# A router and its experts that read x without its norm, in a two-layer recurrent trunk on one core

## The reference, cut to what is computed

```python
def rmsnorm(x, g, eps=RMS_EPS):
    xf = x.astype(jnp.float32)
    y = xf * lax.rsqrt(jnp.mean(xf * xf, axis=-1, keepdims=True) + eps)
    return (y * g.astype(jnp.float32)).astype(x.dtype)
...
def moe_swiglu(h, router, wg, wu, wd):
    probs = jax.nn.softmax((h @ router).astype(jnp.float32), axis=-1)
    top_p, top_i = lax.top_k(probs, TOP_K)
    top_p = top_p / jnp.sum(top_p, axis=-1, keepdims=True)
    gates = jnp.sum(jax.nn.one_hot(top_i, N_EXPERTS, dtype=jnp.float32) * top_p[..., None], axis=-2)
    out = jnp.zeros_like(h)
    for e in range(N_EXPERTS):
        out = out + gates[..., e:e + 1].astype(h.dtype) * swiglu(h, wg[e], wu[e], wd[e])
    return out
...
        h = rmsnorm(x, W['norm_ffn'][i])
        j = i // 2
        if i % 2 == 0:
            x = x + swiglu(h, W['ffn_w_gate'][j], W['ffn_w_up'][j], W['ffn_w_down'][j])
        else:
            x = x + moe_swiglu(h, W['moe_router'][j], W['moe_w_gate'][j], W['moe_w_up'][j],
                               W['moe_w_down'][j])
```

## Time and profile before

| what | value |
|---|---|
| median of 3 runs | 1668.62 us (1667.72 to 1671.55) |
| profiled execution, its own time | 1666.78 us |
| its span, first to last instruction | 1664.9 us |
| mean granted TensorE clock | 0.868 of full |
| busy share PE, PEld, DVE, ACT, POOL | 88, 76, 55, 45, 8% |
| HBM read, written | 225.5 MB, 8.1 MB |
| instructions | 27200 |

### The profile page before, as it was taken

The page is one execution under the profiler, slowest core; times in us unless marked ns, Lnnn a source line. Parts: engine busy times, 40 slices in busy tenths (PEclk is TensorE's granted clock), DMA queues, the critical chain, the costliest instruction groups (busy, mean ns, idle before and its releaser), DMA issues.

```text
span 1664.9 us, 27200 instructions
## 1 busy us (share of the span) xinstructions
PE 1460.6 (88%) x10452; PEld 1257.3 (76%) x10452; DVE 917.4 (55%) x1433; ACT 755.6 (45%) x1124; POOL 127.5 (8%) x160
## 2 busy tenths in 40 slices
PE   4988799897699999899788989766899999999996
PEld 3876677766699999788577776666587788778874
DVE  3644453425444444564445243543588888888885
ACT  4532323123343333462132221432477777877774
POOL 0111111010000000001201100000000000000000
PEclk9997886767899999898788676686799999999998
DMA  5321211014244444042121101320489778987981
GB/s 199 111 65 57 65 39 53 2 66 169 90 152 131 150 150 142 34 124 60 51 64 52 53 2 66 137 87 13 158 296 342 279 285 304 330 286 290 341 287 61
DMA packets 62055, 234.83 MB, mean 141 GB/s; under 512 B 7056, under 2 KB 7152, under 8 KB 61072
## 3 DMA queue, kind: packets, MB, share of 16 engines
q1 hardware_dynamic: 59328, 217.61, 38.0%
q0 software_dynamic: 2496, 13.71, 2.2%
q10 hardware_dynamic: 144, 2.28, 0.3%
HBM read 225.48 MB, written 8.09 MB: 140 GB/s over the span
## 4 chain that ended last, share of the span: by engine, by line
PE 52%; issue 33%; DVE 8%; ACT 4%; POOL 1%; DMA 1%; POOLq 0%; ACTq 0%; DVEq 0%
PE bank L492 11%; PE bank L493 10%; PE bank L494 10%; PE bank L486 7%; ACT whi L1141 1%; PE bank L506 1%; PE bank L604 1%; DVE wlo L1541 1%; PE bank L622 1%; PE bank L636 1%; PE bank L899 1%; PE bank L850 1%; DVE htmp L1556 1%; DMA x<-in_x 1%; PE bank L634 1%
## 5 line engine op out<-in xcount | busy, mean ns | idle before, releaser
L1541 DVE TENSOR_TENSOR wlo<-wraw,whi 128x1024 fp32r<-128x1024 f32 x410 | 506.5, 1238 | 345.3 <-ACT whi L1141 335.2
L1141 ACT ACTIVATE whi<-wraw 128x1024 fp32r<-128x1024 f32 x410 | 433.3, 1060 | 388.9 <-PE bank L494 294.0
L492 PE MATMUL bank<-hh,whi 128*128 128x320 f32 x968 | 333.6, 345 | 53.9 <-DVE hl L1561 36.6
L493 PE MATMUL bank<-hl,whi 128*128 128x320 f32 x968 | 321.7, 332 | 0.0
L494 PE MATMUL bank<-hh,wlo 128*128 128x320 f32 x968 | 319.9, 330 | 0.0
L492 PEld LDWEIGHTS bank<-hh,whi 128*128 128x128 f32 x968 | 202.8, 209 | 69.7 <-issue 43.3
L493 PEld LDWEIGHTS bank<-hl,whi 128*128 128x128 f32 x968 | 202.6, 209 | 0.8
L494 PEld LDWEIGHTS bank<-hh,wlo 128*128 128x128 f32 x968 | 202.2, 209 | 0.0
L1059 PE MATMUL bank<-whi,hh 128*128 128x512 f32 (+1 forms) x384 | 149.3, 389 | 1.0 <-DVE place L2072 1.0
L1061 PE MATMUL bank<-wlo,hh 128*128 128x512 f32 (+1 forms) x384 | 144.2, 376 | 0.0
L1060 PE MATMUL bank<-whi,hl 128*128 128x512 f32 (+1 forms) x384 | 144.1, 375 | 0.0
(11 more groups left out here) (377 smaller groups left out, 2127.1 us busy)
## 6 DMA issues: line engine op xcount, KB each, us to landing
wraw<-in_w SPq DMA_DIRECT2D x410, 512.0 KB, 5.0
smb<-in_s_ssm POOLq DMA_DIRECT2D x2, 1536.0 KB, 6.7
out_o_ssm<-smb POOLq DMA_DIRECT2D x2, 1536.0 KB, 5.4
cst<-in_consts ACTq DMA_DIRECT2D x1, 2225.0 KB, 12.3
srw<-in_s_rwkv POOLq DMA_DIRECT2D x2, 768.0 KB, 6.1
out_o_rwkv<-srw POOLq DMA_DIRECT2D x2, 768.0 KB, 3.6
x<-in_x SPq DMA_DIRECT2D x1, 1280.0 KB, 12.1
out_y<-x SPq DMA_DIRECT2D x1, 1280.0 KB, 4.5
```

What stands on the lines that cost most here:

```text
L492: mm(out, hi, rh, start=first, stop=False)
L493: mm(out, hi, rl, start=False, stop=False)
L1141: af(whi[:, ring % HI, :], wraw[:, POS[ring], :], ACT.Copy).then_inc(S("slot_hi"), 1)
L1541: tt(wlo[:, POS[ring], :], wraw[:, POS[ring], :], whi[:, ring % HI, :].bitcast(F32), ALU.subtract).then_inc(S("slot_split"), 1)
```

## The change

Only layer 1 from the output projection on.

* **No norm in front of the router.** ACT writes `hidh` = x g (rounded) and DVE `hidl` = x g - hidh during the output projection (`raw`, `raw_lo`); router and transposes read them, k by k. The squares are summed per token (`token_sums`: squares as weights, one column of ones, three blocks) into `rs_tok`, the factor r per token. DVE multiplies the logits by it.
* **Ranks and places token by token.** Ranks come from the logits, not from the softmax; `chosen` is rank < 1.5. TensorE counts places with the `causal` and `ones` matrices over `chosen` (`places`, 6 + 3 fp32 matmuls, between the fourth and fifth transpose unit). DVE multiplies by `chosen` into `pos9`. Exp and the gates come after the branch's inputs. The zero fills of the last block are left out, as the gather reads 64 rows there.
* **Per expert, in the loop.** Before the down slots three transposes turn `pick` into the place matrix (B[6]), DVE copies it to `place` at slot 23 and writes the next `pick` at slot 25. After the gather three matmuls of two columns (`slot_scales`) give each slot's gate x r and r; ACT copies them to `slot_g`. Silu uses r as its scale, the down result gate x r.
* ACT's and DVE's split of the third expert slot moves behind the router; the waits for the state DMAs move to DVE, in front of the first pick.
* The dense branch, not taken here, norms x itself.

The diff's core:

```diff
+            def token_sums(i, tiles):
+                for k in tiles:
+                    pe.wait_ge(S("sq_ready"), KT * i + k + 1)
+                    for q, (c0, n) in enumerate(BLOCKS):
+                        m = mm(B[q][0:n, 0:1], sqb[:, k % 2, c0:c0 + n], C("ones", 0, 1), start=(k == 0), stop=(k == KT - 1))
                     m.then_inc(S("sq_used"), 1)
...
             def router():
-                full_slot(G_FFN[L] - 1, G_FFN[L] - 1, B[6][:, 0:T])
+                pe.wait_ge(S("slot_split"), G_FFN[L])
+                for k in range(KT):
+                    pe.wait_ge(S("h_split"), KT * (2 * L + 1) + k + 1)
+                    m = three(B[6][:, 0:T], k, G_FFN[L] - 1, hidh[:, k, :], hidl[:, k, :], k == 0, k == KT - 1)
+                m.then_inc(S("slot_used"), 1)
+                token_sums(2 * L + 1, [KT - 1])
...
                 for u in range(6):
-                    if u >= 2:
-                        pe.wait_ge(S("ro_act"), (2, 3, 5, 6)[u - 2])
+                    if u < 2:
+                        pe.wait_ge(S("nrm_sd"), 2 * L + 2)
+                    else:
+                        pe.wait_ge(S("ro_act"), u)
+                    if u == 4:
+                        places()
...
+            def places():
                 pe.wait_ge(S("ro_dve"), 2)
+                of = [rt["chosen"][0:n, q, :] for q, (_, n) in enumerate(BLOCKS)]
+                for q, (_, n) in enumerate(BLOCKS):
+                    for r in range(q):
+                        mm(B[5][0:n, q * NEXP:(q + 1) * NEXP], C("ones", 0, n), of[r], start=(r == 0), stop=False)
+                    mm(B[5][0:n, q * NEXP:(q + 1) * NEXP], C("causal", 0, n, slice(0, n)), of[q], start=(q == 0), stop=True)
...
+            def slot_scales(i):
+                for q, (_, n) in enumerate(BLOCKS):
+                    of = gate_rs[0:n, q, :, i] if isinstance(i, int) else \
+                        gate_rs[0:n, q, :, bass.ds(i, 1)].rearrange("p a o -> p (a o)")
+                    m = mm(B[1][:, 256:258], pick[0:n, q, :].bitcast(F32), of,
+                           start=(q == 0), stop=(q == 2))
...
             def experts_picked():
-                gather(0)
-                for e in range(NEXP):
-                    for q in range(3):
-                        m = mm(B[5][:, e:e + 1], pick[:, e, q, :].bitcast(F32), rt["g"][:, q, e:e + 1],
-                               start=(q == 0), stop=(q == 2))
-                m.then_inc(S("ro_pe"), 1)
-                for e in range(NEXP):
-                    if e >= 2:
-                        pe.wait_ge(S("ro_dve"), 6 + e - 1)
-                    mm(B[e % 2][:, 0:T], one_of(e, NEXP), pos1[:, :],
-                       start=True, stop=True).then_inc(S("ro_pe"), 1)
+                pe.wait_ge(S("ro_dve"), 4)
+                pe.wait_ge(S("ro_act"), 7)
+                gather()
+                pe.wait_ge(S("ro_dve"), 6)
+                slot_scales(0)
...
+                    for q, (c0, n) in enumerate(BLOCKS):
+                        m = pe.transpose(B[6][:, c0:c0 + n], pick[0:n, q, :].bitcast(F32),
+                                         C("ident", 0, n, slice(0, n)))
+                    m.then_inc(S("place_pe"), 1)
                     for f in range(FT):
...
-                    gather(i + 1)
+                    pe.wait_ge(S("place_in"), 2 * i + 2)
+                    gather()
+                    slot_scales(i + 1)
```

On ACT and DVE:

```diff
+            def raw(tiles):
+                for k in tiles:
+                    act.wait_ge(S("out_read"), KT * L + k + 1)
+                    af(hidh[:, k, :], x[:, k, :], ACT.Copy, scale=V("g_ffn", k)).then_inc(S("hh_k"), 1)
+                    squares(2 * L + 1, [k])
...
+            def slot_scales(i):
+                act.wait_ge(S("taken"), 3 * i + 3)
+                if not isinstance(i, int):
+                    act.wait_ge(S("y_lo"), 2 * i)
+                af(slot_g[:, :], B[1][:, 256:258], ACT.Copy).then_inc(S("taken_hi"), 1)
...
-                            af(sil[:, c % 2, 0:n], B[c % 2][:, 0:n], ACT.Silu).then_inc(S("sil"), 1)
+                            if c == 0:
+                                act.wait_ge(S("taken_hi"), 2 * i + 2)
+                            af(sil[:, c % 2, 0:n], B[c % 2][:, 0:n], ACT.Silu,
+                               scale=slot_g[:, 1:2]).then_inc(S("sil"), 1)
...
+            def raw_lo(k):
+                v.wait_ge(S("hh_k"), KT * (2 * L + 1) + k + 1)
+                stt(hidl[:, k, :], x[:, k, :], V("g_ffn", k), hidh[:, k, :].bitcast(F32), ALU.mult, ALU.subtract)\
+                    .then_inc(S("h_split"), 1)
...
+            def picks(e):
+                at = pos9[:, :, e:e + 1] if isinstance(e, int) else pos9[:, :, bass.ds(e, 1)]
+                return tt(pick[:, :, :], rep(count_up[:, :], 3), at.to_broadcast([P, 3, P]), ALU.is_equal)
...
+                        if j == 2 * FT + 1:
+                            v.wait_ge(S("place_pe"), i + 1)
+                            cp(place[:, :], B[6][:, 0:T]).then_inc(S("place_in"), 1)
+                        if j == 2 * FT + 3:
+                            picks(i + 1).then_inc(S("place_in"), 1)
```

More of the change, by code:

```diff
@@ L365, in trunk @@
         htk = [sb("htk_" + k, [P, 3, D], F32R) for k in "hl"]
[L366 to L370, removed]
+        pick = sb("pick", [P, 3, P], F32R)
+        exp_end, top[0] = top[0], yt_at
         cmp = sb("cmp", [P, 3, NEXP, NEXP])
@@ L970, in router @@
                 m.then_inc(S("ro_pe"), 1)
[L971 to L978, removed]
+                pe.wait_ge(S("ro_act"), 9)
                 for e in range(NEXP):
@@ L1009, in experts_dense, with gather @@
                 expert_loop(pe, L, body)
-            def gather(i):
+            def gather():
                 for z, bk in enumerate((6, 2)):
                     for k in range(KT):
-                        for q in range(3):
[L1016 to L1019, removed]
-                    m.then_inc(S("taken"), 1)
@@ L1122, in _ @@
                 else:
+                    norm(2 * l + 1, range(KT - 2, KT))
+                    pe.wait_ge(S("h_split"), KT * (2 * l + 2))
                     ffn(l)
@@ L1514, in _ @@
                 else:
+                    squares(2 * l + 1, [KT - 1])
+                    norm(2 * l + 1)
                     act.wait_ge(S("st_out"), 16 * 5 * (l + 1))
@@ new lines, in by_block @@
+            def by_block(*tiles):
+                last = BLOCKS[2][1]
+                return [[t[:, 0:2, :] for t in tiles], [t[0:last, 2:3, :] for t in tiles]]
+            def router():
+                v.wait_ge(S("nrm_sd"), 2 * L + 2)
+                step(v.reciprocal(rs_tok[:, :], rs_tok[:, :]))
+                v.wait_ge(S("ro_pe"), 1)
+                logits, rs8 = B[7][:, 0:3 * NEXP].rearrange("p (q e) -> p q e", e=NEXP), over(rs_tok[:, :], NEXP)
+                for to, a, b in by_block(rt["l"], logits, rs8):
+                    m = tt(to, a, b, ALU.mult)
+                step(m)
+                l_, e_, p_, rk = (rt[k][:, :, :] for k in ("l", "e", "p", "rank"))
+                step(v.tensor_reduce(rt1[:, :, 0], l_, AX.X, ALU.max))
+                tt(p_, l_, over(rt1[:, :, 0], NEXP), ALU.subtract).then_inc(S("ro_dve"), 1)
+                all4 = [P, 3, NEXP, NEXP]
+                of_j, of_e = l_.unsqueeze(2).to_broadcast(all4), l_.unsqueeze(3).to_broadcast(all4)
+                lower = C("before").rearrange("p (e j) -> p e j", j=NEXP).unsqueeze(1).to_broadcast(all4)
+                step(tt(cmq[:, :, :, :], of_j, of_e, ALU.is_equal))
+                tt(cmp[:, :, :, :], of_j, of_e, ALU.is_gt)
+                step(tt(cmq[:, :, :, :], cmq[:, :, :, :], lower, ALU.mult))
+                step(tt(cmp[:, :, :, :], cmp[:, :, :, :], cmq[:, :, :, :], ALU.add))
+                step(v.tensor_reduce(rk, cmp[:, :, :, :], AX.X, ALU.add))
+                ts(rt["chosen"][:, :, :], rk, 1.5, None, ALU.is_lt).then_inc(S("ro_dve"), 1)
+                v.wait_ge(S("ro_pe"), 6)
+                step(v.tensor_reduce(n_most[:, 0:1], B[5][0:1, 32:32 + NEXP], AX.X, ALU.max))
+                cp(n_most_i[:, :], n_most[:, 0:1]).then_inc(S("ro_dve"), 1)
+                v.wait_ge(S("ro_dve"), 2)
+                upto = B[5][:, 0:3 * NEXP].rearrange("p (q e) -> p q e", e=NEXP)
+                for to, a, b in by_block(pos9[:, :, 0:NEXP], upto, rt["chosen"]):
+                    m = tt(to, a, b, ALU.mult)
+                step(m)
+                v.wait_ge(S("st_out"), 16 * 5 * (L + 1))
+                v.wait_ge(S("ring_out"), 16 * 3 * (L + 1))
+                picks(0).then_inc(S("ro_dve"), 1)
```

220 lines of the change are left out of this document (105 added, 115 removed).

## The result

| | before | after |
|---|---|---|
| median, lowest to highest, us | 1668.17 (1664.19 to 1671.55) | 1711.68 (1708.35 to 1713.59) |
| span of the profiled execution | 1664.9 | 1710.8 |
| mean granted TensorE clock | 0.868 | 0.849 |

The change is slower: ratio 1.0265, 95% interval 1.0248 to 1.0282, four runs of each. The forecast was 1620, and the range ended at 1633.

A forecast was written before the change was run, and what follows sets the result against it. TensorE was taken as the bound: little used or at half clock before the first expert, full in the expert passes. Front -56.9 plus loop +8.2 gave -48.7 us, from 1668.62 to 1620; range 1612 to 1633.

The forecast's parts named there:

- From the gather to the first expert: Front: gather 5.4 us at full clock, then scales for one expert; 7.0 us instead of 36.5, 29.5 saved.
- Up to the logits: Front, projection to router's logits: no wait for the norm, 14.4 us saved, less 0.4 for the token sums.
- Logits to gather: Front, after the router: gather starts 10.5 us behind the logits instead of 21.3, 10.8 us saved.
- C: Before the first gather: the branch is dear on TensorE, up to +3.9 us, 1624; chance included in the forecast's 0.55.
- E: Logits to gather: transpose units and ACT's copies set the pace, counts queue behind; +7 us, 1627; chance 0.07.
- Whether the clock holds: Front, transposes and counts before the first gather: gaps at most 1.3 us, so full clock was expected to hold.
- rival A: Front: the clock falls before the first gather; gather, scales and ramp cost +8.3 us, 1628; chance 0.20.
- the rule on transposes: Before the first gather: full clock does not engage for transposes, so the gather would start at half clock, 1628.
- the ramp: First expert pass: starting at half clock cost 2.6 us before; starting at full clock would save it.
- The loop: Each expert pass: transposes 0.55, scales net 0.33, DVE's additions 0.15, together 1.03 us; times 8, +8.2.
- Rival B: Expert loop: DVE's additions in full and half of the 0.42 us wait not returned; +9 us, 1629; chance 0.13.
- Rival D: Expert loop: small matmuls throw the clock down in every pass, 8.2 us each, +66, 1686; chance 0.02.

The follow-up runs named there:

- e1: The change, but its gather reads all 128 rows of the third token block, the missing rows zeroed by ACT: 1621.6 us, ratio to before 0.9723.
- e4: The change with its alternating gather, but two of three scale matmuls and two of three pick transposes per pass left out: 1696.2 us, one run.
- e3: The change with 64-row matmuls kept but grouped: in each gather half first the 16 of 128 rows, then the 8 of 64: 1642.81 us.
- e2: The kernel before, with only its gather reading 64 rows in the last block: 1747.58 us, one run.
- e7: The change with block order third, first, second for odd k, so 8 changes of row count per gather half instead of 16: 1680.78 us.
- e8: e1 with the three slot_scales matmuls of each pass issued three times, same result: 1645.91 us.
- e10: e1 with the first half of each gather issued twice, same result: 1643.86 us.
- e9: e1 with slot_scales issued twice in each pass, same result: 1632.42 us.

## Why the prediction was wrong

**The step that failed** is "From the gather to the first expert": "5.4 at full clock (in a pass its first half is 2.79)", and, by the same assumption, the loop's sum, which charges the gather of each pass nothing. Both carried the duration of 128-row matmuls over to a gather that reads 64 rows for its last block. The edit was seen, described as zero fills left out, and priced as a saving on ACT; its other side, every third matmul of another shape, was given no term and no bound. The Trainium skill (TensorEngine Tiling (Array Packing), Tiling Modes) says that changing the tiling mode, not just the tile, drains TensorE, and lists 64 rows by 128 columns as a mode of its own. The runs fit this: a stop of 0.14 us a change at full clock and 0.18 to 0.19 at half, 32 changes a gather. That the mode of the array changes there is not itself recorded in them. Only about half of what was lost is the stops; the other half is the clock.

Point by point, from the rows of the change:

* **Up to the logits.** From the projection's first matmul, the logits are done in 41.0 us (1070.84 to 1111.87), 54.0 before: 13.0 saved, 14.0 forecast. The sums of a tile take 0.70 us (0.65 forecast), and TensorE waits 1.47 us for the squares of the last tile but one.
* **Logits to gather.** 10.6 us, 10.5 forecast. Rivals C and E fell: the gather waits for ACT's copy, not for the branch.
* **Gather to first expert.** 17.2 us against 7.0 forecast; e1 has 7.0 (1122.99 to 1130.00). The arithmetic was right for the gather it assumed.
* **Whether the clock holds, rival A.** In the change the clock fell only with the gather running: 1.00 from 1104 to 1122, 0.86 over the next 2 us, 0.50 from 1124 to 1140. e1 did the gather at full clock right behind the transposes, so A fell, and with it the rule on transposes that stands beside it: TensorE had done mostly transposes from 1113 to 1122, and the clock was 1.00. But e1's first expert began at full clock and its matmuls are at half 0.8 us later. From its start to the next gather it takes 51.20 us, 1.6 more than the later ones, where the kernel before paid 2.6: 1.0 us of the ramp came back, not all of it.
* **The loop.** Three transposes 0.58 us (0.55 forecast); the scales 0.79 up to the first put (0.75); the wait in front of the sixth put is gone, as said. A pass of e1 is 58.4, +1.1 (1.03 forecast). Rival B fell. TensorE's matmuls wait for no `wlo` in e1's pass, and its weight loads wait 0.7 us for it, as before.
* **Rival D** had 0.02. Of its sum, "the rest of the gather (up to 5.4), the scales 0.65 and the ramp 2.6", the gather (2.5 for half clock in its second half) and the scales (0.7) came true, with puts at half clock (+1.7) besides. The ramp didn't: in the loop the expert's matmuls took 0.1 to 0.6 us more than e1's, not 2.6. Its trigger was wrong (e4), and what spoke against it, "today's gather, 5.4 us long, leaves the clock at 1.00", is true of a gather that this change no longer has.

Where the time went: the first expert starts 41.05 us earlier. (It would be 43.0, but the projection itself began 2.0 later, at 1070.84 instead of 1068.86; the kernels that share the change's code up to there begin their first gather anywhere from 1118.28 to 1123.49, so I read nothing into it.) Each pass is 11.0 us longer, which makes 88 in eight. The difference, 47, is about the 45.9 by which the span grew. Of the 11.0, 1.1 is the work added. The other 9.9 can be read part by part, the pass from 1534.40 beside one of e1, from start to start. The first half of the gather is 2.2 longer, at full clock, so these are stops. The second half is 5.1 longer; where it ran at half clock from its start it was 5.5, of which 3.0 are 16 stops and 2.5 is the clock. The scales are 0.7 longer, the puts 1.7 and the expert's matmuls 0.1.

**Left open.** Why e3's clock fell in some passes and not in others wasn't settled: each half of its gathers is 0.2 to 0.3 us longer than e1's while the clock holds, and they differ otherwise only in the order and in the 64 rows of 16 matmuls; which of these did it wasn't tried. e2 and e4 were run once each; their times are 76 and 61 us above what the rivals allowed (1672 and 1635), where the runs of one kernel differ by 9 us at most here.

## What to carry to other kernels

When a change takes rows off an operand to spare a fill, price the matmuls too: compare the shape of each with its neighbour's, since a series that alternates between 128 and 64 rows pays at each change (here 0.14 us beside 0.11 of work). Filling the rows with zeros was worth 90 us here for two ACT instructions; an order that halves the changes (e7) gave back 31. And read the granted clock beside the busy row: where a stretch without dense matmuls gets slower or longer, add a little of the same work and see whether the clock holds, as e8 to e10 do.

## What the runs showed that I had not expected

* A matmul of 64 rows costs what one of 128 does (2.94 us for a half with 8 of them, 2.79 without), while a change of row count costs more than the matmul itself.
* "Busy" hides it: during the stops TensorE is busy for 2.00 of 2.00 us. The number of instructions in the window (12 where 17 fit) and the length of the group tell, and so does the row of the weight loads: they are busy for 1.51 of 2.00 us there, and for 2.00 of 2.00 in a gather without stops (e10).
* The clock held behind 8.2 us of 128x128 matmuls and 0.9 of two-column ones (e10), and fell in four of seven passes behind 5.5 us of the first and 1.7 of the second (e9). Work added to the gather cost its own time; work added to the scales cost more than its own.
